# Latent attention: the maxima of a pair of heads taken ahead of the sums of the pair before

## The chip, the cores and the metric
The kernel runs on one core of a Trainium2 chip. The metric is the time of one execution on the device in microseconds (us), the median of a few runs.

## What is computed
The reference is a trunk of four residual layers over 256 tokens of width 1024 in float32: RMSNorm, a token mixer, RMSNorm, a SwiGLU channel mixer with 2816 hidden columns. The mixers are stick-breaking attention (layers 0 and 3), multi-head latent attention (layer 1) and sliding-window attention (layer 2). The change touches layer 1 alone:

```
def block(args):                      # 16 heads, CHUNK = 64
    logits = (einsum('bqhd,bshd->bhqs', qn, k_nope) + einsum('bqhr,bsr->bhqs', qr, k_rope)) * scale
    logits = where(key_chunk[None, :] <= q_chunk[:, None], logits, NEG_INF)
    p = softmax(logits, axis=-1)
    return einsum('bhqs,bshd->bqhd', p, v)
```

and the result of the heads goes through the output projection `w_o` and is added to x.

## The kernel before
All products of weights are made on TensorE in three passes: a weight unit w (128 x 2048 float32, 1 MB) is taken apart into a high part `w_hi` (ScalarE, L458) and a low part `w_lo = raw - w_hi` (VectorE, L783). There are 183 such units besides the first three, streamed through three slots. SyncE loads unit u into slot u mod 3 once VectorE has taken the low part of unit u-3; TensorE waits for `lo_done`. In the code both engines call this step `split(u)`. Units b to b+7 of layer 1 (b is its first unit) are projections down and up, units b+8 to b+11 its output projection.

The engines run programs written out by hand, one queue for each engine in program order, tied by semaphores. In layer 1 the 16 heads go as 8 pairs, p = 0 to 7. For a pair there are these steps:

- TensorE `logits(p)`: mask, early queries (128 keys) and late queries (256 keys) of both heads into one of two double banks. It waits for `exps(p-2)`, which empties that double bank.
- VectorE `maxima(p)`: two reductions from the banks (L984, L985) and the scaled negative (L987).
- ScalarE `exps(p)`: four exponentials into `scratch` (L599). They wait for `maxima(p)`.
- VectorE `sums(p)`: two reductions over `scratch` (L994, L996) and the reciprocal (L998). They wait for `exps(p)`.
- GpSimd `mla_products`: four scalings of the exponentials in place (L387). They wait for the reciprocal.
- TensorE `transposes(p)`: three for each of two heads (L1500) into the one double bank 3. They wait for the copy of the pair before, the first three for two of the four products, the second three for all four.
- ScalarE `copy_pt(p)`: the transposed weights to SBUF (L607).
- TensorE `values(p)` (L1515): waits for the copy and for the low part of the output of pair p-2.
- ScalarE `out_hi(p)` (L612), VectorE `lo(p)` (L857): high and low part of the pair's output, in `o_split`.

TensorE's round is `transposes(p)`, `logits(p+3)`, `values(p-1)`; in round 0 `queries(7)` (24 tile products ending a projection) stands in between, in rounds 5 and 6 four tiles of the output projection follow, and in round 7 two. Below, "the projection's start" is the first tile of the output projection, behind `values(4)`. VectorE's `queries(7)` (L959) moves the last two heads' queries out of the bank. Before the rounds come `exps(0)` to `exps(2)`, `maxima(0)`, `maxima(1)`, `sums(0)`, `sums(1)`.

The first loop below is ScalarE's round, the second VectorE's:

```
                for p in range(PAIRS_OF_HEADS):
                    copy_pt(p)
                    if p >= 1:
                        out_hi(p - 1)
                    exps(p + 3)
...
                    sums(p + 2)
                    maxima(p + 3)
                    if p >= 1:
                        lo(p - 1)
                    if p in (2, PAIRS_OF_HEADS - 3):
                        split(b + 9 if p == 2 else b + 10)
```

The order of the instructions on each engine is this text; no planner moves anything.

Of the kernel before, what the change touches and what calls it, by code (L numbers as in the profile page):

```python
# [38 lines left out]
PAIRS_OF_HEADS = HEADS // 2  # L39
# [65 lines left out]
def trunk(nc, w, x_in, consts, gains, bv, rel_rows, rel_scratch, out):  # L105
    ctx = ExitStack()
    with ctx:
# [76 lines left out]
        def mla_scores(p):  # L184

            return two_banks[2 - p % 2][:, :].rearrange("p (a s) -> p a s", a=2)

        def mla_weights(p):
            return scratch[:, 768 * (p % 4):768 * (p % 4) + 768].rearrange("p (a s) -> p a s", a=2)

        def mla_turned(p):
            return turned[:, p % 2, :].rearrange("p (a s) -> p a s", a=2)

        def mla_out(p):
            return bank[(p + 1) % 2]
# [247 lines left out]
        def _(act):  # L443
# [7 lines left out]
            def split(u):  # L451

                if u >= UNITS:
                    return
                slot = u % RAW_SLOTS
                act.wait_ge(raw_loaded[slot], 16 * (u // RAW_SLOTS))
                act.wait_ge(unit_used, u - SPLIT_SLOTS + 1)
                act.activation(w_hi[slot][:, :], raw[slot][:, :], ACT.Copy).then_inc(hi_done, 1)  # L458
# [13 lines left out]
            def first_guess(s, count, first, last):  # L472

                act.wait_ge(s.ms, count)
                t = step(act.activation(guess[:, first:last], ms[:, first:last], ACT.Ln))
                act.wait_ge(act_step, t)
                act.activation(guess[:, first:last], guess[:, first:last], ACT.Exp, scale=-0.5).then_inc(s.guess, 1)
# [72 lines left out]
            def latent_attention(i):  # L550
                m, b, n, c = mixer[i], MIXER_BASE[i], 2 * i, latent

                def latent_hi(k):
                    act.wait_ge(c.c_new, k // 2 + 1)
                    act.activation(lat_hi[:, k, :], lat[:, k, :], ACT.Identity,
                                   scale=vec[:, G_CQ + k:G_CQ + k + 1]).then_inc(c.hi, 1)

                split(b + 3)
                first_guess(norm, n + 1, 0, SEQ + TOKEN_SUMS[n])
                for k in (0, 1, 3):  # L560
                    latent_hi(k)
                split(b + 4)
                first_guess(c, 1, SEQ, 514)
                for k in (4, 5):
                    latent_hi(k)

                act.wait_ge(m.krope_sum, 1)
                act.activation(k_all[HD:P, 0, :], bank[0][HD:P, 0:SEQ], ACT.Copy).then_inc(m.krope_new, 1)
                act.wait_ge(m.krope_new, 1)
                act.dma_start(k_all[HD:P, 1:HEADS, :],  # L570
                              k_all[HD:P, 0:1, :].to_broadcast([HD, HEADS - 1, SEQ])).then_inc(m.kfill, 16)
                split(b + 5)

                def value_part(t, half):

                    if t and half:
                        act.wait_ge(unit_used, b + 5)
                    else:
                        act.wait_ge(m.v_part, 2 * t + half + 1)
                    act.activation(v_all[:, t, 512 * half:512 * half + 512], bank[MLA_V_BANKS[2 * t + half]][:, :],  # L580
                                   ACT.Identity, scale=rstd_c[:, 512 + t:513 + t]).then_inc(m.v_new, 1)

                act.wait_ge(c.rstd, 1)
                value_part(0, 0)
                first_guess(c, 2, 0, SEQ)
                value_part(0, 1)
                split(b + 6)
                value_part(1, 0)
                value_part(1, 1)
                split(b + 7)  # L590

                def exps(p):
                    if p >= PAIRS_OF_HEADS:
                        return
                    pr, s, lg = mla_weights(p), small[:, p % 4, :], mla_scores(p)
                    act.wait_ge(m.max_new, 3 * p + 3)
                    for late, keys in enumerate((slice(0, P), slice(P, 384))):
                        for a in range(2):
                            act.activation(pr[:, a, keys], lg[:, a, keys], ACT.Exp,  # L599
                                           bias=s[:, 4 + 2 * late + a:5 + 2 * late + a],  # L600
                                           scale=MLA_SCALE).then_inc(m.exp_new, 1)

                def copy_pt(p):
                    act.wait_ge(m.pt, p + 1)
                    if p >= 2:
                        act.wait_ge(m.av, p - 1)
                    act.activation(mla_turned(p), two_banks[3][:, :].rearrange("p (a s) -> p a s", a=2)[:, :, 0:384],  # L607
                                   ACT.Copy).then_inc(m.pt_new, 1)

                def out_hi(p):  # L610
                    act.wait_ge(m.av, p + 1)
                    act.activation(o_hi[:, p, :], mla_out(p)[:, 0:SEQ], ACT.Copy).then_inc(m.o_hi, 1)  # L612

                split(b + 8)
                exps(0)
                exps(1)
                split(b + 9)
                exps(2)
                for p in range(PAIRS_OF_HEADS):
                    copy_pt(p)  # L620
                    if p >= 1:
                        out_hi(p - 1)
                    exps(p + 3)
                    if p == PAIRS_OF_HEADS - 3:
                        split(b + 10)
                out_hi(KT - 1)
                out_projection(i)
# [133 lines left out]
            for i in range(DEPTH):  # L761
                (stick_breaking, latent_attention, window_attention)[i % 3](i)
                swiglu(i)
# [4 lines left out]
        def _(dve):  # L768
# [8 lines left out]
            def split(u):  # L777

                if u >= UNITS:
                    return  # L780
                slot = u % RAW_SLOTS
                dve.wait_ge(hi_done, u + 1)
                dve.tensor_tensor(w_lo[slot][:, :], raw[slot][:, :], w_hi[slot][:, :].bitcast(FP32),  # L783
                                  ALU.subtract).then_inc(lo_done, 1)
# [127 lines left out]
            def latent_attention(i):  # L912
                m, b, n, c = mixer[i], MIXER_BASE[i], 2 * i, latent
# [63 lines left out]
                def maxima(p):  # L977
                    if p >= PAIRS_OF_HEADS:
                        return
                    s, lg = small[:, p % 4, :], mla_scores(p)  # L980
                    dve.wait_ge(m.logits, p + 1)
                    if p >= 4:
                        dve.wait_ge(m.p_new, 4 * (p - 3))
                    dve.tensor_reduce(s[:, 0:2], lg[:, :, 0:P], AX_X, ALU.max).then_inc(m.max_new, 1)  # L984
                    dve.tensor_reduce(s[:, 2:4], lg[:, :, P:384], AX_X, ALU.max).then_inc(m.max_new, 1)  # L985
                    dve.wait_ge(m.max_new, 3 * p + 2)
                    dve.tensor_scalar(s[:, 4:8], s[:, 0:4], -MLA_SCALE, None, ALU.mult).then_inc(m.max_new, 1)  # L987

                def sums(p):
                    if p >= PAIRS_OF_HEADS:  # L990
                        return
                    s, pr = small[:, p % 4, :], mla_weights(p)
                    dve.wait_ge(m.exp_new, 4 * p + 2)
                    dve.tensor_reduce(s[:, 8:10], pr[:, :, 0:P], AX_X, ALU.add).then_inc(m.sum_new, 1)  # L994
                    dve.wait_ge(m.exp_new, 4 * p + 4)
                    dve.tensor_reduce(s[:, 10:12], pr[:, :, P:384], AX_X, ALU.add).then_inc(m.sum_new, 1)  # L996
                    dve.wait_ge(m.sum_new, 2 * p + 2)
                    dve.reciprocal(s[:, 12:16], s[:, 8:12]).then_inc(m.inv_new, 1)  # L998

                def lo(p):  # L1000
                    dve.wait_ge(m.o_hi, p + 1)
                    out_lo(m, o_lo[:, p, :], mla_out(p)[:, 0:SEQ], o_hi[:, p, :])
# [7 lines left out]
                queries(5)  # L1010
                queries(6)
                sums(1)
                maxima(2)
                split(b + 8)
                for p in range(PAIRS_OF_HEADS):
                    if p == 1:
                        queries(7)
                    sums(p + 2)
                    maxima(p + 3)
                    if p >= 1:  # L1020
                        lo(p - 1)
                    if p in (2, PAIRS_OF_HEADS - 3):
                        split(b + 9 if p == 2 else b + 10)
                lo(KT - 1)
                out_projection(i)

# [810 lines left out]
```

## Time and profile before

| | |
|---|---|
| median of 3 runs | 1195.81 us (1195.05 to 1196.33) |
| the profiled execution: own time | 1196.22 us |
| its span, first to last instruction | 1194.2 us |
| TensorE busy | 98% of the span |
| VectorE, ScalarE, GpSimd busy | 68%, 53%, 24% |
| mean granted clock of TensorE | 0.996 |

The span is the part of the execution that the trace shows; the profiled execution's own time is about 2 us more. Times in the rows below count from the start of the span. A matmul's end is modelled, so the starts are the safer numbers. A row of the timeline may merge several equal instructions (xN), and then its length is that of the whole group.

### The profile page before, as it was taken

Reading aid. Unit: us, or ns where it says so; the run is one execution under the profiler, and the core shown is the slowest. Engines: PE = TensorE matmul, PEld = TensorE weight load, DVE = VectorE, ACT = ScalarE, POOL = GpSimd, SP = SyncE. Lnnn points to the kernel's source line nnn. Section 1 sums busy time; section 2 is a strip of 40 time slices with the busy share of each in tenths; the row PEclk is TensorE's granted clock in tenths of the full one; section 3 lists DMA queues with packets and bytes.
Section 4 is the critical chain, followed back from the end, with each engine's and each line's share of the span. In section 5 each row is a group of like instructions: output and inputs, shape, how many; then the busy total and the mean of one; then the engine's idle time right before and its main releaser. Section 6 shows DMA issues by size and latency. Waiting matters only on the chain.

```text
span 1194.2 us, 18227 instructions
## 1 busy us (share of the span) xinstructions
PE 1168.3 (98%) x7410; PEld 1040.5 (87%) x7410; DVE 810.5 (68%) x857; ACT 628.3 (53%) x763; POOL 286.5 (24%) x290
## 2 busy tenths in 40 slices
PE   8999999999999999999999999999999999999996
PEld 6988888888998888888899888888889888888885
DVE  7686767775588667776556577766556867777653
ACT  5675565554354555554436545555346755555531
POOL 5000542211123343221101153221110005422221
PEclk9999999999999999999999999999999999999999
DMA  9733545555552345555543245555545324455541
GB/s 314 217 121 106 176 177 180 180 206 194 186 174 89 114 160 212 180 182 206 194 156 107 82 170 212 183 201 201 187 160 193 106 106 177 177 193 187 196 165 35
DMA packets 30828, 201.84 MB, mean 169 GB/s; under 512 B 3504, under 2 KB 4592, under 8 KB 7328
## 3 DMA queue, kind: packets, MB, share of 16 engines
q1 hardware_dynamic: 28800, 197.41, 46.9%
q0 software_dynamic: 352, 1.31, 0.9%
q10 hardware_dynamic: 1600, 2.02, 0.7%
q8 instruction: 58, 0.95, 0.3%
q14 instruction: 18, 0.15, 0.0%
HBM read 197.91 MB, written 1.84 MB: 167 GB/s over the span
## 4 chain that ended last, share of the span: by engine, by line
PE 89%; DVE 8%; ACT 2%; DMA 0%; issue 0%; DVEq 0%; ACTq 0%
PE banks L1209 39%; PE banks L1213 21%; PE banks L1203 6%; PE banks L1205 6%; PE banks L1204 6%; PE banks L1197 4%; DVE w_lo L783 3%; DVE x_split L798 2%; PE banks L1338 1%; PE banks L1280 1%; PE banks L1352 1%; PE banks L1582 1%; DVE w_lo L792 1%; PE banks L1610 0%; ACT w_hi L458 0%; PE banks L1340 0%
## 5 line engine op out<-in xcount | busy, mean ns | idle before, releaser
L783 DVE TENSOR_TENSOR w_lo<-raw,w_hi 128x2048 fp32r<-128x2048 f32 x183 | 450.4, 2461 | 214.0 <-ACT w_hi L458 213.9
L458 ACT ACTIVATE w_hi<-raw 128x2048 fp32r<-128x2048 f32 x183 | 349.3, 1909 | 97.0 <-PE banks L1213 47.2
L1209 PE MATMUL banks<-x_split,w_hi 128*128 128x512 f32 x1408 | 339.1, 392 | 5.5 <-DVE x_split L798 5.4
L1209 PEld LDWEIGHTS banks<-x_split,w_hi 128*128 128x128 f32 x1408 | 258.6, 188 | 58.7 <-DVE x_split L798 8.9
L1213 PEld LDWEIGHTS banks<-x_split,w_lo 128*128 128x128 f32 x1408 | 181.8, 192 | 6.9
L1213 PE MATMUL banks<-x_split,w_lo 128*128 128x256 f32 x1408 | 184.0, 284 | 0.0
L1209 PE MATMUL banks<-hid_split,w_hi 128*128 128x512 f32 x704 | 173.2, 392 | 0.0
L1209 PEld LDWEIGHTS banks<-hid_split,w_hi 128*128 128x128 f32 x704 | 127.4, 188 | 23.3
L1203 PE MATMUL banks<-x_split,w_hi 128*128 128x256 f32 x384 | 110.3, 287 | 0.0
L1204 PE MATMUL banks<-x_split,w_hi 128*128 128x256 f32 x384 | 108.6, 283 | 0.0
L1205 PE MATMUL banks<-x_split,w_lo 128*128 128x256 f32 x384 | 108.6, 283 | 0.0
L353 POOL TENSOR_TENSOR scratch<-scratch,rstd 128x512 f32<-128x512 f32 x44 | 57.4, 1305 | 205.8 <-ACT scratch L712 205.8
L356 POOL TENSOR_TENSOR scratch<-scratch 128x512 f32<-128x512 f32 x44 | 71.8, 1631 | 140.2 <-DVE scratch L1122 139.9
L1213 PEld LDWEIGHTS banks<-hid_split,w_lo 128*128 128x128 f32 x704 | 94.0, 191 | 5.8
L338 POOL TENSOR_TENSOR sq<-x 128x256 f32<-128x256 f32 x62 | 57.5, 927 | 163.0 <-DVE x_split L798 127.6
L1213 PE MATMUL banks<-hid_split,w_lo 128*128 128x256 f32 x704 | 95.6, 282 | 0.0
L1203 PE MATMUL banks<-o_split,w_hi 128*128 128x256 f32 x320 | 92.6, 289 | 0.4
L1205 PE MATMUL banks<-o_split,w_lo 128*128 128x256 f32 x320 | 90.5, 283 | 0.0
L1204 PE MATMUL banks<-o_split,w_hi 128*128 128x256 f32 x320 | 90.5, 283 | 0.0
L470 ACT ACTIVATE x_split<-x,vec 128x256 fp32r<-128x256 f32 x64 | 30.7, 503 | 108.9 <-DVE x L1154 81.7
L700 ACT ACTIVATE scratch<-banks 128x512 f32<-128x512 f32 x44 | 26.2, 596 | 115.5 <-PE banks L1213 115.5
L1203 PEld LDWEIGHTS banks<-x_split,w_hi 128*128 128x128 f32 x384 | 73.5, 191 | 2.8 <-issue 2.4
(174 smaller groups left out, 1476.9 us busy)
## 6 DMA issues: line engine op xcount, KB each, us to landing
raw<-w SPq DMA_DIRECT2D x183, 1024.0 KB, 4.9
raw<-w SPq DMA_DIRECT2D x8, 256.0 KB, 6.3
x<-x_in SPq DMA_DIRECT2D x2, 512.0 KB, 5.5
raw<-w SPq DMA_DIRECT2D x2, 512.0 KB, 8.4
out<-x SPq DMA_DIRECT2D x4, 256.0 KB, 2.9
k_all<-k_all ACTq DMA_DIRECT2D x1, 960.0 KB, 10.5
rel_scratch<-rel_lut POOLq DMA_DIRECT2D x1, 768.0 KB, 10.6
rel_bias<-rel_scratch POOLq DMA_DIRECT2D x2, 256.0 KB, 8.5
```

Of the source, the lines that this page charges most:

```text
L338: step(pool.tensor_tensor(dst[:, :], x[:, k, :], x[:, k, :], ALU.mult))
L353: pool.tensor_tensor(gate, gate, both(rstd[:, 0:SEQ]), ALU.mult).then_inc(f.scaled, 1)
L356: pool.tensor_tensor(value, gate, value, ALU.mult).then_inc(f.hid, 1)
L458: act.activation(w_hi[slot][:, :], raw[slot][:, :], ACT.Copy).then_inc(hi_done, 1)
L470: act.activation(x_hi[:, k, :], x[:, k, :], ACT.Identity, scale=gain(n, k)).then_inc(norm.hi, 1)
L783: dve.tensor_tensor(w_lo[slot][:, :], raw[slot][:, :], w_hi[slot][:, :].bitcast(FP32), ALU.subtract).then_inc(lo_done, 1)
L1197: ins = pe.matmul(dst, a, v, start=first and n == 0, stop=last and n == 2, skip_group_check=True)
L1203: pe.matmul(dst, wh, xh, start=first, stop=False, skip_group_check=True)
L1204: pe.matmul(dst, wh, xl, start=False, stop=False, skip_group_check=True)
L1205: return pe.matmul(dst, wl, xh, start=False, stop=last, skip_group_check=True)
L1209: return pe.matmul(pair(b), wt[0], xs, start=first, stop=False, skip_group_check=True)
L1213: return pe.matmul(pair(b)[:, 1, :], wt[1], xs[:, 0, :], start=False, stop=last, skip_group_check=True)
```

## The change
On VectorE each round takes `maxima(p+3)` ahead of `sums(p+2)` instead of behind it, and the round p = -1 takes `maxima(2)` alone. `queries(7)` goes from the start of round 1 to the end of round 0. The low part of unit b+8 goes from ahead of the rounds to the end of round 1, that of b+9 from the end of round 2 to the end of round 3; that of b+10 stays at the end of round 5. On ScalarE `exps(p+3)` goes ahead of `out_hi(p-1)`. No instruction is added or removed, and TensorE's, GpSimd's and SyncE's programs are the same.

```diff
@@ -618,9 +618,9 @@
                 exps(2)
                 for p in range(PAIRS_OF_HEADS):
                     copy_pt(p)
+                    exps(p + 3)
                     if p >= 1:
                         out_hi(p - 1)
-                    exps(p + 3)
                     if p == PAIRS_OF_HEADS - 3:
                         split(b + 10)
                 out_hi(KT - 1)
@@ -1010,17 +1010,16 @@
                 queries(5)
                 queries(6)
                 sums(1)
-                maxima(2)
-                split(b + 8)
-                for p in range(PAIRS_OF_HEADS):
-                    if p == 1:
+                for p in range(-1, PAIRS_OF_HEADS):
+                    maxima(p + 3)
+                    if p >= 0:
+                        sums(p + 2)
+                    if p == 0:
                         queries(7)
-                    sums(p + 2)
-                    maxima(p + 3)
                     if p >= 1:
                         lo(p - 1)
-                    if p in (2, PAIRS_OF_HEADS - 3):
-                        split(b + 9 if p == 2 else b + 10)
+                    if p in (1, 3, PAIRS_OF_HEADS - 3):
+                        split({1: b + 8, 3: b + 9}.get(p, b + 10))
                 lo(KT - 1)
                 out_projection(i)
```

## Rows read from the trace of the kernel before

**Rows 1.** The page, parts 1 and 4: TensorE busy; the chain by engine.
```profile
PE 1168.3 (98%) x7410; PEld 1040.5 (87%) x7410; DVE 810.5 (68%) x857; ACT 628.3 (53%) x763; POOL 286.5 (24%) x290
...
PE 89%; DVE 8%; ACT 2%; DMA 0%; issue 0%; DVEq 0%; ACTq 0%
```

**Rows 2.** Busy time by windows, from pair 1's transposes to the output projection.
```profile
core 0: us, PE busy (x) PEld busy (x) DVE busy (x) ACT busy (x) POOL busy (x), PEclk, DMA share, GB/s
373.88:391.97 18.09, 14.62 (x121) 10.64 (x119) 15.70 (x35) 9.41 (x25) 7.83 (x20) 1.00 0.34 117
```

**Rows 3.** Timeline of TensorE: start us, us, instruction, [idle before, releaser].
```profile
371.30 0.60 PE L1488 MATMUL banks<-k_all,q_all 128*128 128x256 f32 x2
...
373.88 0.81 PE L1500 MATMUL banks<-table,scratch 128*128 128x128 f32 x6
...
376.22 0.87 PE L1515 MATMUL banks<-turned,v_all 128*64 128x256 f32 x8
...
377.76 0.87 PE L1500 MATMUL banks<-table,scratch 128*128 128x128 f32 x6 [0.67 <-ACT turned L607]
...
381.37 0.87 PE L1500 MATMUL banks<-table,scratch 128*128 128x128 f32 x6 [0.34 <-ACT turned L607]
...
385.43 0.87 PE L1500 MATMUL banks<-table,scratch 128*128 128x128 f32 x6 [0.79 <-ACT turned L607]
...
390.36 0.87 PE L1500 MATMUL banks<-table,scratch 128*128 128x128 f32 x6 [1.67 <-ACT turned L607]
...
391.97 0.39 PE L1203 MATMUL banks<-o_split,w_hi 128*128 128x256 f32 x1
```

**Rows 4.** Timeline of VectorE in the same stretch.
```profile
371.10 2.28 DVE L783 TENSOR_TENSOR w_lo<-raw,w_hi 128x2048 fp32r<-128x2048 f32 x1
...
373.30 0.41 DVE L994 TENSOR_REDUCE small<-scratch 128x2 f32<-128x256 f32 x1
...
374.43 0.39 DVE L984 TENSOR_REDUCE small<-banks 128x2 f32<-128x256 f32 x1
...
375.53 0.68 DVE L959 TENSOR_TENSOR q_all<-banks,rope_q 128x512 f32<-128x512 f32 x1
...
383.19 0.41 DVE L857 TENSOR_TENSOR o_split<-banks,o_split 128x256 fp32r<-128x256 f32 x1
...
383.52 2.28 DVE L783 TENSOR_TENSOR w_lo<-raw,w_hi 128x2048 fp32r<-128x2048 f32 x1
```

**Rows 5.** Timeline of ScalarE in the same stretch.
```profile
372.45 0.83 ACT L607 ACTIVATE turned<-banks 128x768 f32<-128x768 f32 x1
...
375.66 1.35 ACT L599 ACTIVATE scratch<-banks,small 128x128 f32<-128x128 f32 x4 [2.37 <-DVE small L987]
...
376.88 0.83 ACT L607 ACTIVATE turned<-banks 128x768 f32<-128x768 f32 x1
...
377.57 0.41 ACT L612 ACTIVATE o_split<-banks 128x256 fp32r<-128x256 f32 x1
```

**Rows 6.** Timeline of GpSimd: the four products of pairs 1 and 2.
```profile
370.00 3.72 POOL L387 TENSOR_SCALAR scratch<-scratch,small 128x128 f32<-128x128 f32 x4 [1.87 <-DVE small L998]
374.61 1.62 POOL L387 TENSOR_SCALAR scratch<-scratch,small 128x128 f32<-128x128 f32 x4 [0.89 <-DVE small L998]
```

**Rows 7.** Timeline in the channel mixer of layer 1: VectorE and GpSimd.
```profile
449.25 2.28 DVE L783 TENSOR_TENSOR w_lo<-raw,w_hi 128x2048 fp32r<-128x2048 f32 x1
...
449.48 3.21 POOL L356 TENSOR_TENSOR scratch<-scratch 128x512 f32<-128x512 f32 x1 [3.51 <-DVE scratch L1122]
```

**Rows 8.** Windows (columns as Rows 2) at the entries of two channel mixers.
```profile
132.00:136.00 4.00, 2.62 (x11) 1.52 (x9) 2.85 (x6) 1.60 (x3) 3.61 (x6) 1.00 0.77 262
...
136.00:138.00 2.00, 1.85 (x9) 1.77 (x10) 0.85 (x2) 1.22 (x1) 1.84 (x3) 0.73 0.00 0
...
138.00:140.00 2.00, 2.00 (x12) 2.00 (x11) 1.54 (x1) 0.00 (x0) 2.00 (x1) 0.50 0.00 0
...
420.00:424.00 4.00, 3.30 (x14) 2.17 (x12) 3.07 (x6) 0.83 (x2) 3.61 (x6) 1.00 0.65 219
```

## The prediction

> **What bounds the kernel now.** I read the page first. TensorE is busy 98% of the span and is 89% of the chain that ended last; loads have no share in it [rows 1]. A reordering in layer 1 can therefore only win what TensorE waits there. The windows give it: from the transposes of pair 1 (373.88) to the projection's start (391.97) TensorE is busy 14.62 of 18.09 us at the full clock, and VectorE 15.70 [rows 2]. The timeline shows where. Each of the transposes of pairs 2 to 5 has idle time ahead of it, released by ScalarE's copy [rows 3]. A round without a wait is as long as transposes, logits and values: 376.22 - 373.88 = 2.34 for the first two and 0.80 for the values, 3.14 us. The last stretch, from 390.36 to 391.97, is 1.61. So 18.09 - 4 x 3.14 - 1.61 = 3.9 us are waits, and that is the most that can be won. Behind 391.97 TensorE has projection tiles between its steps for pairs, and I count nothing there.
>
> Why is the copy late? ScalarE has `exps(p+2)` ahead of `copy_pt(p)`: the copy of pair 1 starts at 376.88, behind the exponentials of 375.66, though its transposes began at 373.88 [rows 3, 5]. Those exponentials waited for maxima that stood behind sums on VectorE: 374.43 behind 373.30, and these behind a low part of 2.2 us at 371.10 [rows 4]. The change cuts this tie. I see it as real: sums of a pair need its exponentials, and the next pair's maxima don't.
>
> **Durations.** Start to next start: sums 1.13 (373.30 to 374.43), maxima 1.10 (374.43 to 375.53), a low part of weights 2.20 (371.10 to 373.30), `lo` 0.33 (383.19 to 383.52) [rows 4]. From the start of maxima to the exponentials 1.25 (374.43 to 375.66, rounded up), exponentials 1.22 (375.66 to 376.88), `out_hi` 0.41 long and its `lo` 0.44 behind its start; a copy 0.70 to the next and 0.88 to the transposes (376.88 to 377.76) [rows 3 to 5]. From sums to the products on GpSimd 1.31 (373.30 to 374.61), and the products 1.62 [rows 4, 6]. Logits: transposes 0.66, then 1.68 to the values, and 1.79 from their start to the maxima, an estimate from 371.30 + 0.60.
>
> **The term that speaks against the change.** The four products of pair 1 took 3.72 us and not 1.62; VectorE's low part of b+8 lay over them, 371.10 to 373.38 [rows 4, 6]. In the channel mixer a GpSimd product started 0.23 behind such a low part and ended 1.29 behind its end (449.48 + 3.21 against 449.25 + 2.28) [rows 7]. So the low part of a unit and a GpSimd instruction exclude one another; what GpSimd has left when it starts comes 2.2 us later. The Trainium skill, "SBUF — State Buffer", section "Who interferes with whom", states this as a rule: one pair of ports is an exclusive lock between GpSimd and a VectorE instruction with two SBUF inputs, held for the whole instruction. The low part reads `raw` and `w_hi`, so by that rule it contends; the trace agrees, with the 3.72 us.
>
> In the kernel before, maxima stand between the sums and the low part of b+9, so its products (of pair 4) are through before 383.52, and the collision of b+8 at 371.10 lies under TensorE's `queries(7)`, which ends only at 373.88. After the change the low parts of b+8 and b+9 stand directly behind sums and `lo`, and the products just released are half done.
>
> **Round by round, after the change.** Logits of pair 3 end at 371.90, so `maxima(3)` starts 371.93 and `exps(3)` 373.18 (375.66 before). `sums(2)` 373.03, products of pair 2 374.34 to 375.96, `queries(7)` 374.16 to 374.85. This last is moved at no cost: VectorE then idles for the logits of pair 4, which start 0.66 behind TensorE's 373.88.
> Round 1: `copy_pt(1)` waits for its transposes, 374.73; values(0) 376.22; transposes(2) 377.02 (377.76 before, gain 0.74). `maxima(4)` 376.33, `exps(4)` 377.59, `sums(3)` 377.47, products(3) from 378.78. `out_hi(0)` stands behind the exponentials, 378.82, so `lo(0)` 379.26, and the low part of b+8 comes at 379.59, where two of four products are through. They end at about 382.7, behind 381.8 to 382.2 when the low part ends. That is the first collision.
> Round 2: TensorE could start transposes(3) at 380.17 and has the first three; the second three wait until 382.8. Logits(6) 383.2, values(2) 384.9. VectorE has `maxima(5)` only at 381.85 and `exps(5)` is at 383.08, `sums(4)` 382.95, products(4) 384.26 to 385.88. `copy_pt(3)` comes behind `out_hi(1)` at 384.58.
> Round 3: transposes(4) 385.69 (385.43 before), the second three at 386.0; logits(7) 386.4, values(3) 388.1. `maxima(6)` 385.08, `exps(6)` 386.33, `sums(5)` 386.20, products(5) from 387.51; `out_hi(2)` 387.56, `lo(2)` 388.00, low part of b+9 388.33 to 390.6 or, behind a third product, 390.95. Second collision: the products end at 391.4.
> Round 5: transposes(5) may start at 388.9, but the second three wait for the last product, 391.5. Values(4) 391.9, the projection's start 392.7. Before it was 391.97 [rows 3]: **0.7 us later.**
>
> Behind that everything TensorE asks for is ready: `maxima(7)` 390.6 and `exps(7)` 391.85, products(6) to 394.6 for transposes asked for at 395.7, products(7) hit by the low part of b+10 (396.25) until 399.1, against 400.2. The first tiles of the projection want `o_lo` of pair 3 at 394.9 and have it at 393.9. So its rhythm, and all behind it, moves as one.
>
> **Moved edits that cost nothing.** The low part of b+8 ends 8.5 us later and that of b+9 about 5 later, and SyncE's loads of b+11 and of the next mixer's first unit with them. TensorE needs b+8 at the projection's start and b+9 some 4.5 us on; b+11 follows behind all of both, far over 10 us later. With the late ends of 382 and 391 there are 10 and 6 us to spare; without that cover each us of lateness would be one of the end. GpSimd has no DMA in layer 1, so its queue carries only products. `out_hi` behind the exponentials delays `lo(p-1)` by 1.2 us, and values of pair p+1 wait for it; in round 2 they start at 384.9 with `lo(0)` done at 379.6. The queue behind the waiting `lo` is the low part, 0.66 us in round 1 and 0.67 in round 3; only by that do two products get through first.
>
> **The unknown prices.** How the lock goes at a tie: the third product first or the low part first. It moves the end of the low part by 0.4 and the products' end hardly, so +0.4 to +1.3 for the forecast with my rounding of each step. Whether the second product pair is held: if all four got through, round 5's wait would be gone; if none did, transposes(5) start late as a whole, 0.3 more.
>
> **Rivals.**
> No collision that binds (18%): GpSimd's products slip through before the low part, as in the kernel before at 383.52, because `lo` waits longer than I have it. It decides if the low part of b+9 starts 0.8 us later than 388.33. Transposes(3) would be whole at 380.2, transposes(4) at 385.46 (VectorE's 2.2 us at b+8 still delay `exps(5)`), transposes(5) 388.8 with all products at 389.13, the projection at 390.35: -1.6 us, 1194.2.
> Full pipelining (4%): maxima stay so far ahead that all waits go, -3.9 us, 1191.9. VectorE speaks against it, 15.70 of 18.09 us busy, with both low parts still in the stretch [rows 2].
> A fall of TensorE's clock (16%): the clock granted was 0.73 and 0.50 in 136 to 138 and 138 to 140 us, behind a stretch in which TensorE was busy 2.62 of 4 us; a like entry at 420 to 424 with 3.30 of 4 kept 1.00 [rows 8]. The fall took (1 - 0.73) x 2 + (1 - 0.50) x 2 = 1.5 us of matmul time at least. The change makes two waits of 2.3 us where the longest was 1.67 [rows 3]; if one of them brings the half clock to the projection, that is 0.7 + 1.5 = +2.2, 1198.0, and two falls, or one whole with the late tie, +2.6 to +3.8. It decides if the granted clock is under 1 between 383 and 397. Against it: at 388.7 the wait of 1.67 did nothing.
> The change does nothing (10%): both orders meet the same last wait, within 0.3 of before. Near the forecast in time, and not to be told from it but by the trace.
>
> **How the numbers follow.** The forecast, two collisions and +0.4 to +1.3, has 52%. Profiled execution: 1196.22 with a span of 1194.2, so 1196.9 and 1194.9 after. The median before was 0.4 lower than the profiled one; I put 0.7 on the median: 1195.81 + 0.7 = 1196.5. The range takes in the no-collision case below with the runs' own spread of 0.6, and one clock fall above with the same: 1193.7 to 1198.8. A measurement tells about 0.2%, 2.4 us, from no change. Faster by that needs over 60% of all waits gone: full pipelining and a small part of the no-collision case, 5%. Slower by that: the worse part of the clock case, 10%. The same 85%.
>
> **What the profile after would show.** Products of pairs 3 and 5 at 3.6 to 3.9 us and that of pair 4 at 1.62: the collisions. `exps(3)` 2.5 us earlier: the cut tie. TensorE's longest idle inside the transposes of pairs 3 and 5, its releaser no longer ScalarE's copy but GpSimd's product; the projection's start near 392.7. I am wrong if that start is before 391.5 (the products weren't held or not waited for), or if it is after 394 (a wait that I don't see), or if the clock falls there.

## The result and the profile after

Measured together, 20 runs of each: the kernel before 1195.12 us in the median (1194.43 to 1196.75), the changed kernel 1196.94 us (1195.71 to 1199.30). The ratio is 1.0014, with a 95% interval of 1.0008 to 1.0020: 1.7 us slower, inside what the prediction called the same, and inside its range. The profiled execution took 1198.20 us, its span 1196.3 us.

The page after has GpSimd on the chain that ended last, with 1%, where it had no share [rows 1]:

```profile
PE 1171.4 (98%) x7410; PEld 1042.7 (87%) x7410; DVE 809.8 (68%) x857; ACT 628.7 (53%) x763; POOL 291.9 (24%) x290
...
PE 90%; DVE 7%; ACT 2%; POOL 1%; DMA 0%; issue 0%; DVEq 0%; ACTq 0%
```

The stretch from the transposes of pair 1 to the projection's start, by windows (columns as in [rows 2]). It was 18.09 us and is 20.11, and VectorE's work in it is nearly the same, 15.61 us against 15.70 [rows 2]. TensorE is busy 16.70 us for the work that took 14.62, at a mean clock of 0.90:

```profile
373.07:393.18 20.11, 16.70 (x120) 11.69 (x118) 15.61 (x32) 9.55 (x25) 10.71 (x16) 0.90 0.20 64
```

The same stretch on TensorE's timeline answers to [rows 3]:

```profile
373.07 0.82 PE L1499 MATMUL banks<-table,scratch 128*128 128x128 f32 x6
...
376.21 0.87 PE L1499 MATMUL banks<-table,scratch 128*128 128x128 f32 x6
...
379.41 0.55 PE L1499 MATMUL banks<-table,scratch 128*128 128x128 f32 x3
381.75 0.55 PE L1499 MATMUL banks<-table,scratch 128*128 128x128 f32 x3 [1.79 <-POOL scratch L387]
...
386.23 0.87 PE L1499 MATMUL banks<-table,scratch 128*128 128x128 f32 x6
...
389.43 0.55 PE L1499 MATMUL banks<-table,scratch 128*128 128x128 f32 x3
391.59 0.55 PE L1499 MATMUL banks<-table,scratch 128*128 128x128 f32 x3 [1.61 <-POOL scratch L387]
...
393.18 0.58 PE L1202 MATMUL banks<-o_split,w_hi 128*128 128x256 f32 x1
```

The reader is to see two things. Transposes of pair 2 follow at once, without the 0.67 of before. And those of pairs 3 and 5 are cut in two halves of three, with a wait in between that a GpSimd product ends. The copy from ScalarE ends no wait any more. VectorE's, ScalarE's and GpSimd's timelines of the changed kernel show why:

```profile
378.78 2.30 DVE L783 TENSOR_TENSOR w_lo<-raw,w_hi 128x2048 fp32r<-128x2048 f32 x1
381.01 0.41 DVE L984 TENSOR_REDUCE small<-banks 128x2 f32<-128x256 f32 x1
...
388.62 2.30 DVE L783 TENSOR_TENSOR w_lo<-raw,w_hi 128x2048 fp32r<-128x2048 f32 x1
```

```profile
372.39 1.35 ACT L599 ACTIVATE scratch<-banks,small 128x128 f32<-128x128 f32 x4
373.93 0.81 ACT L607 ACTIVATE turned<-banks 128x768 f32<-128x768 f32 x1 [0.19 <-PE banks L1499]
```

```profile
377.96 3.73 POOL L387 TENSOR_SCALAR scratch<-scratch,small 128x128 f32<-128x128 f32 x4 [2.77 <-DVE small L998]
383.44 1.62 POOL L387 TENSOR_SCALAR scratch<-scratch,small 128x128 f32<-128x128 f32 x4 [1.74 <-DVE small L998]
387.81 3.73 POOL L387 TENSOR_SCALAR scratch<-scratch,small 128x128 f32<-128x128 f32 x4 [2.74 <-DVE small L998]
...
395.41 3.76 POOL L387 TENSOR_SCALAR scratch<-scratch,small 128x128 f32<-128x128 f32 x4 [0.50 <-DVE small L998]
```

`exps(3)` comes 0.68 us ahead of the start of transposes(1) where it came 1.78 behind it [rows 3, 5]: 2.5 us sooner. The low parts of 378.78 and 388.62 lie over the products of pairs 3 and 5, which take 3.73 us; those of pair 4 take 1.62. The last line is pair 7's products, held by the low part of b+10 as the prediction had it; TensorE asks for them only at 401.87 and doesn't wait. The granted clock (columns as in [rows 2]) is what the single timelines don't say:

```profile
376.00:380.00 4.00, 3.96 (x35) 2.74 (x31) 3.36 (x7) 2.33 (x6) 2.04 (x3) 1.00 0.03 6
380.00:384.00 4.00, 2.25 (x12) 1.88 (x13) 3.37 (x8) 1.75 (x6) 2.26 (x4) 0.78 0.42 123
384.00:388.00 4.00, 4.00 (x28) 2.79 (x28) 2.62 (x7) 1.96 (x6) 1.26 (x4) 0.79 0.33 139
388.00:392.00 4.00, 2.38 (x18) 1.40 (x17) 3.68 (x6) 0.96 (x2) 3.54 (x4) 1.00 0.00 0
392.00:396.00 4.00, 4.00 (x23) 3.40 (x22) 2.98 (x9) 3.90 (x8) 2.22 (x6) 0.57 0.76 266
```

This trace had no fall of the clock at the entry of layer 0's channel mixer, where that of before had one [rows 8], but one of 10 to 14 us from the span's start, and its layer 1 starts 0.8 us sooner. Below I therefore count from the start of transposes(1), which the change doesn't move (it stands 4.39 us behind that of transposes(0) in both traces), to the projection's start and to the end of the span. "Falls" are stretches of lower clock behind transposes(1), the last 12 us of the span left aside; in windows of 2 us the granted clock goes down to 0.50 to 0.56 in each of them, the lower of its two levels (1.2 and 2.4 GHz). The kernels of the table are explained in the next section.

| kernel | to the projection | to the end | falls | ratio to before, 95% |
|---|---|---|---|---|
| before | 18.09 | 820.3 | 0 | |
| changed | 20.11 | 823.2 | 2 | 1.0014 (1.0008 to 1.0020) |
| changed, again | 20.87 | 823.5 | 2 | |
| old places | 18.02 | 820.1 | 1 | 0.9993 (0.9985 to 1.0002) |
| one input | 18.05 | 820.1 | 1 | 0.9999 (0.9990 to 1.0008) |
| ScalarE as before | 18.22 | 820.3 | 0 | 1.0008 (1.0000 to 1.0017) |
| filler 16 | 21.49 | 823.5 | 0 | 1.0029 (1.0019 to 1.0039) |
| filler 8 | 18.68 | 822.4 | 1 | 1.0014 (1.0005 to 1.0023) |
| filler 8, again | 18.68 | 820.7 | 0 | |
| b+9 away | 16.58 | 819.1 | 0 | 0.9995 (0.9986 to 1.0004) |
| before, colliding | 19.50 | 821.5 | 1 | 1.0008 (0.9999 to 1.0017) |
| before, 0.7 us more | 18.98 | 821.1 | 0 | 1.0009 (1.0000 to 1.0018) |
| clear | 14.41 | 816.9 | 0 | 0.9975 (0.9966 to 0.9984) |
| clear, b+9 early | 14.41 | 818.8 | 1 | 0.9973 (0.9962 to 0.9984) |

Each count stands for one profiled execution; the ratios stand for 7 to 20 timed runs of the kernel, and 0.0010 of them is 1.2 us.

### The profile page after: what moved, and what is told of

Read it like the earlier page. It is cut to its first block, busy times and chain, and to the rows that moved or that the text cites. A ratio compares the mean times of both kernels' runs of the same rounds, so it can differ in the third digit from the quotient of the medians.

```text
span 1196.3 us, 18227 instructions
## 1 busy us (share of the span) xinstructions
PE 1171.4 (98%) x7410; PEld 1042.7 (87%) x7410; DVE 809.8 (68%) x857; ACT 628.7 (53%) x763; POOL 291.9 (24%) x290
## 4 chain that ended last, share of the span: by engine, by line
PE 90%; DVE 7%; ACT 2%; POOL 1%; DMA 0%; issue 0%; DVEq 0%; ACTq 0%
PE banks L1208 39%; PE banks L1212 21%; PE banks L1202 6%; PE banks L1204 6%; PE banks L1203 6%; PE banks L1196 4%; DVE w_lo L783 2%; DVE x_split L798 2%; PE banks L1337 1%; PE banks L1279 1%; PE banks L1351 1%; PE banks L1581 1%; POOL scratch L387 1%; DVE w_lo L792 1%; PE banks L1487 1%; PE banks L1609 0%
## 5 line engine op out<-in xcount | busy, mean ns | idle before, releaser
L338 POOL TENSOR_TENSOR sq<-x 128x256 f32<-128x256 f32 x62 | 61.7, 996 | 163.0 <-DVE x_split L798 127.6
```

Source lines behind the costliest of these rows:

```text
L338: step(pool.tensor_tensor(dst[:, :], x[:, k, :], x[:, k, :], ALU.mult))
```

## The experiments

All of them change layer 1 alone.

**Old places.** The changed order, with the low parts of b+8 and b+9 where they were.

```diff
                 for p in range(-1, PAIRS_OF_HEADS):
                     maxima(p + 3)
+                    if p == -1:
+                        split(b + 8)
...
-                    if p in (1, 3, PAIRS_OF_HEADS - 3):
-                        split({1: b + 8, 3: b + 9}.get(p, b + 10))
+                    if p in (2, PAIRS_OF_HEADS - 3):
+                        split(b + 9 if p == 2 else b + 10)
```

> The changed order of maxima and sums, with the low parts of b+8 and b+9 where they were (ahead of round 0, and at the end of round 2). Lock theory (a low part and GpSimd's products exclude one another, and TensorE waits for the held products): the products of pair 4 take 3.7 us, those of pairs 3 and 5 1.6 us; one wait of TensorE on a product instead of two; the projection's start 1.6 us earlier than before, so -1.6 us against before, or about 0 if the clock falls behind that one wait. Theory that the order of maxima and sums itself costs: slower than before by 1 to 2 us, as the changed kernel is. Theory that ScalarE's order costs: the same, 1 to 2 us slower.

GpSimd's and TensorE's timelines of this kernel:

```profile
377.54 1.63 POOL L387 TENSOR_SCALAR scratch<-scratch,small 128x128 f32<-128x128 f32 x4 [1.48 <-DVE small L998]
380.79 3.74 POOL L387 TENSOR_SCALAR scratch<-scratch,small 128x128 f32<-128x128 f32 x4 [1.62 <-DVE small L998]
```

```profile
384.59 0.55 PE L1501 MATMUL banks<-table,scratch 128*128 128x128 f32 x3 [1.85 <-POOL scratch L387]
```

One collision that TensorE waits for, with pair 4, and one wait; transposes(5) follow at 389.07. With one fall of the clock behind the wait, the projection starts 18.02 us behind transposes(1), and not 16.5. The order of maxima and sums itself costs nothing: the ratio is 0.9993 (0.9985 to 1.0002). Its lowest three runs, 1192.93 to 1193.19, are 1.2 us under the lowest of before (1194.10), which is about what a run without that fall would give.

**One input.** The low parts of b+8 and b+9 are not computed; a reduction over `raw` of the same length stands in their place.

```diff
+                def one_input(u):
+                    slot = u % RAW_SLOTS
+                    dve.wait_ge(hi_done, u + 1)
+                    dve.tensor_reduce(w_lo[slot][:, 0:1], raw[slot][:, :], AX_X, ALU.max).then_inc(lo_done, 1)
...
-                    if p in (1, 3, PAIRS_OF_HEADS - 3):
-                        split({1: b + 8, 3: b + 9}.get(p, b + 10))
+                    if p in (1, 3):
+                        one_input(b + 8 if p == 1 else b + 9)
+                    if p == PAIRS_OF_HEADS - 3:
+                        split(b + 10)
```

> The changed kernel, but the low parts of b+8 and b+9 are not computed: a reduction over raw of the same 2048 columns stands in their place, with one SBUF input instead of two and the same waits and signals. Lock theory: all products take 1.6 us, TensorE no longer waits for a product, the clock stays at 1.00, and the kernel is 1.6 us faster than before (3.4 us faster than the changed one). Theory that only VectorE's queue counts (2.2 us ahead of maxima 5 and 7 whatever the instruction is): no change against the changed kernel, +1.8 us against before.

VectorE's, GpSimd's and TensorE's timelines and one window:

```profile
379.74 2.27 DVE L1003 TENSOR_REDUCE w_lo<-raw 128x1 fp32r<-128x2048 f32 x1
```

```profile
378.92 1.63 POOL L387 TENSOR_SCALAR scratch<-scratch,small 128x128 f32<-128x128 f32 x4 [2.76 <-DVE small L998]
384.37 1.63 POOL L387 TENSOR_SCALAR scratch<-scratch,small 128x128 f32<-128x128 f32 x4 [3.81 <-DVE small L998]
387.62 1.63 POOL L387 TENSOR_SCALAR scratch<-scratch,small 128x128 f32<-128x128 f32 x4 [1.62 <-DVE small L998]
```

```profile
385.57 1.39 PE L1506 MATMUL banks<-table,scratch 128*128 128x128 f32 x6 [1.93 <-POOL scratch L387]
```

```profile
384.00:388.00 4.00, 2.43 (x12) 2.10 (x13) 2.85 (x9) 3.08 (x10) 2.01 (x6) 0.74 0.53 221
```

The instruction in the low part's place begins as far behind the sums and is as long (2.27 us), yet products(3) and (5) take 1.63 us. So it is not VectorE being busy that shuts GpSimd out. The reduction is also another operation and writes one column where the low part writes 2048; that neither of these makes the difference is seen in the kernel before, where `queries(7)` (375.53 to 376.21), a TENSOR_TENSOR with one input from the bank `banks` and one from SBUF that writes 512 columns, lay over the products of pair 2, and they took 1.62 us [rows 4, 6]. What is left is the second input from SBUF. That much of the expectation held. The gain of 1.6 us did not come: the ratio is 0.9999. The 2.2 us ahead of `maxima(5)` and `sums(4)` are still there, products(4) start only at 384.37, and TensorE waits 1.93 us for them; behind that wait the clock fell in this trace, and the stretch is 18.05 us, 1.6 longer than the 16.5 of the prediction's no-collision case. That case had the wait too (transposes(4) at 385.46, which is 11.58 us behind transposes(1); here 11.54), but gave the fall no place in it.

**ScalarE as before.** The changed kernel with `out_hi(p-1)` ahead of `exps(p+3)`.

```diff
                     copy_pt(p)
-                    exps(p + 3)
                     if p >= 1:
                         out_hi(p - 1)
+                    exps(p + 3)
```

> The changed kernel with ScalarE's order as before (out_hi ahead of the exponentials). Lock theory: lo comes up to 0.8 us earlier and the low parts with it, so that they hold three products or four instead of two; the waits on products stay, two of 1.5 to 2.3 us; 0 to -0.7 us against the changed kernel, +1 to +2 against before. Theory that ScalarE's order costs: the loss against before goes, +0.3 or less.

```profile
377.04 3.66 POOL L387 TENSOR_SCALAR scratch<-scratch,small 128x128 f32<-128x128 f32 x4 [2.76 <-DVE small L998]
...
385.38 3.66 POOL L387 TENSOR_SCALAR scratch<-scratch,small 128x128 f32<-128x128 f32 x4 [1.81 <-DVE small L998]
```

```profile
380.04 0.52 PE L1499 MATMUL banks<-table,scratch 128*128 128x128 f32 x3 [1.49 <-POOL scratch L387]
```

(GpSimd's and TensorE's timelines.) The low part starts at 377.17, 0.13 us behind the products, and they are held almost whole, but it is over sooner too, and at each of the two pairs TensorE waits some 1.5 us ahead of the first three transposes and 0.2 ahead of the second, where it waited 1.79 and 1.61. From transposes(1) to the projection 18.22 us, no fall in this trace. In the runs it is 0.7 us better than the changed kernel, with overlapping intervals. The interval, 1.0000 to 1.0017, holds both what the lock theory expected against before (+1 to +2 us) and what the theory on ScalarE's order did (+0.3 or less), so the runs don't decide. In the traces the order is worth 0.5 us against filler 8 below, which has the same two collisions and no fall in layer 1 either (18.22 against 18.68); the rest of the 1.9 us to the changed kernel's 20.11 comes with the falls.

**Filler 16 and filler 8.** More matmuls in both waits, so that TensorE is not idle there.

```diff
                     for a in range(2):
+                        if a == 1 and p in (3, 5):
+                            for _ in range(FILL):
+                                pe.matmul(bank[6][:, 384:512], ident, x[:, 0, 0:P], start=True, stop=True)
                         pe.wait_ge(m.p_new, 4 * p + 2 * a + 2)
```

> The changed kernel with 16 more matmuls of 128 columns (about 1.8 us, into columns that nobody reads) ahead of the second three transposes of pairs 3 and 5, that is inside TensorE's two waits on products. Clock theory (half of the loss is not the waits but the half clock behind them): the clock stays at 1.00 in this stretch, the waits on the product shrink to some 0.3 us, and the kernel is 1 to 1.5 us faster than the changed one, +0.3 to +0.9 against before, with a smaller spread of its runs. Theory that the waits alone cost: no change or up to 0.3 us slower than the changed kernel.

```profile
380.52 3.74 PE L1500 MATMUL banks<-x,table 128*128 128x128 f32 x32
```

(TensorE's timeline.) I had sized them by the transposes, six in 0.66 us. They take twice that, 3.74 us for 16, longer than the waits. So the kernel is slower than the changed one, 1.0029, and not the 1 to 1.5 us faster that were expected. The trace says one thing: with TensorE busy the clock stayed at 1.00 through layer 1. With 8 of them the size is right:

> As the filler kernel, with 8 matmuls instead of 16: they took 3.74 us for 16, so 1.9 us for 8, which lies inside the waits of 2.1 to 2.3 us. Clock theory: granted clock 1.00 in layer 1, the projection's start 0.7 to 0.9 us later than before counted from the transposes of pair 1, and so +0.7 to +0.9 against before, 0.9 to 1.1 us faster than the changed kernel. Theory that the waits alone cost: as the changed kernel, +1.8.

> The kernel with 8 filler matmuls in each wait once more. Clock theory: granted clock 1.00 from 376 to 400 us again, and the loss that is left over 0.7 us stands at an entry of a channel mixer.

The windows of the second profile of filler 8 in layer 1, then the one of its first profile, in layer 3, where the clock fell:

```profile
380.00:384.00 4.00, 4.00 (x35) 3.63 (x34) 3.90 (x7) 1.13 (x4) 2.31 (x2) 1.00 0.25 57
384.00:388.00 4.00, 4.00 (x31) 2.68 (x31) 2.82 (x8) 3.08 (x9) 2.31 (x6) 1.00 0.49 207
...
392.00:396.00 4.00, 4.00 (x38) 3.70 (x32) 2.49 (x7) 4.00 (x7) 2.71 (x7) 1.00 0.59 242
```

```profile
1002.00:1008.00 6.00, 5.53 (x25) 5.07 (x26) 3.40 (x3) 3.27 (x3) 4.84 (x5) 0.72 0.19 37
```

Both traces have 18.68 us to the projection, 0.6 more than before, and no fall in layer 1. One has none later either and ends 0.4 us over before (820.7 against 820.3); the other has one at layer 3's channel mixer and ends 1.7 us later. So in the traces the rest of the changed kernel's loss, 2.5 and 2.8 us (823.2 and 823.5 against the 820.7 of the filler without any fall), comes with its two falls. The timed runs don't follow: I had expected filler 8 to be 0.9 to 1.1 us faster than the changed kernel, and its ratio is the same 1.0014. Its mean clock over 11 runs is 0.9957, that of before 0.9956 and that of the changed kernel 0.9947.

**The changed kernel again**, for the place of its falls.

> The changed kernel once more, for where its clock falls. Clock theory: granted clock under 1 once or twice between 382 and 396 us, as in its first profile. If these falls are chance, none here.

```profile
380.00:384.00 4.00, 2.87 (x13) 2.44 (x14) 3.09 (x8) 2.34 (x6) 2.25 (x6) 0.64 0.57 186
384.00:388.00 4.00, 4.00 (x30) 2.81 (x28) 2.41 (x7) 1.80 (x6) 1.07 (x3) 0.93 0.18 76
388.00:392.00 4.00, 2.21 (x17) 1.30 (x18) 3.97 (x7) 0.86 (x3) 3.11 (x3) 0.92 0.14 23
392.00:396.00 4.00, 4.00 (x25) 3.29 (x26) 2.56 (x7) 4.00 (x8) 2.63 (x7) 0.65 0.63 244
```

Again two falls, in nearly the same two stretches. I don't take their places for chance. But not every run can have had both as they are here. In all 14 traces transposes(1) start at 372.1 us or later, so a run with both falls would have a span of at least some 372.1 + 823.2 = 1195.3 us (an estimate); 11 of the 20 timed runs of the changed kernel have a shorter one, 1193.6 to 1195.0. Both profiled executions, 1196.3 and 1196.0, are from its slower half.

**Before, 0.7 us more.** The kernel before with three more matmuls ahead of the projection.

```diff
                         pe.wait_ge(m.exp_new, 4 * 7)
+                        for _ in range(3):
+                            pe.matmul(bank[4][:, 0:P], ident, x[:, 0, 0:P], start=True, stop=True)
                         out_part(i, 0, range(0, 4))
```

> The kernel before with three more matmuls of 128 columns (0.7 us, result not read) ahead of the output projection's first tile in layer 1: the same lateness at the projection's start as the changed kernel's own, with none of its waits. Theory that the loss is the lateness and the clock falls in layer 1: +0.7 us in the median against before, mean clock as before. Theory that any such shift moves the later entries of the channel mixers to where the clock falls more often: +1.5 to +2.2 us in the median, though TensorE's added work is 0.7 us; the lowest run at +0.7.

```profile
390.71 0.94 PE L1538 MATMUL banks<-x,table 128*128 128x128 f32 x6
391.40 0.36 PE L1203 MATMUL banks<-o_split,w_hi 128*128 128x256 f32 x1
```

(TensorE's timeline.) They take 0.69 us; the other 0.2 of the stretch's 0.89 came ahead of them, at transposes(2), where TensorE waited 0.86 instead of 0.67. The trace ends 0.8 us later, with no fall; the lowest run is 1195.06 against 1194.10, and the ratio 1.0009 with 1.0000 to 1.0018. That spans both expectations, 0.7 us and 1.5 or more. Inconclusive on whether a shift of this size brings more falls at later entries.

**b+9 away.** The changed kernel with the low part of b+9 at the end of round 5 and that of b+10 at the end of round 6.

```diff
-                    if p in (1, 3, PAIRS_OF_HEADS - 3):
-                        split({1: b + 8, 3: b + 9}.get(p, b + 10))
+                    if p in (1, 5, 6):
+                        split({1: b + 8, 5: b + 9}.get(p, b + 10))
```

> The changed kernel with only the low part of b+9 moved away, to the end of round 5 (b+10 to the end of round 6). Lock theory: the products of pair 5 take 1.6 us, those of pair 3 stay at 3.7; one wait on a product instead of two; the projection's start 1.6 us earlier than before, with one fall of the clock behind the first wait 0 against before, without it -1.6. Theory that the first collision (b+8) makes the loss: as the changed kernel, +1 to +2.

```profile
382.38 0.55 PE L1499 MATMUL banks<-table,scratch 128*128 128x128 f32 x3 [1.79 <-POOL scratch L387]
```

(TensorE's timeline.) One wait is left, at transposes(3), and the stretch is 16.58 us, 1.5 shorter than before, where 1.6 were expected without a fall. The ratio, 0.9995 (0.9986 to 1.0004), is between the two numbers, 0 and -1.6 us. Against the changed kernel's 1.0014 the second collision carries the loss: what the first one costs is less than what the new order gains by pair 5.

**Before, colliding.** The kernel before, with the low part of b+9 between the sums of pair 4 and the maxima of pair 5.

```diff
                     sums(p + 2)
+                    if p == 2:
+                        split(b + 9)
                     maxima(p + 3)
                     if p >= 1:
                         lo(p - 1)
-                    if p in (2, PAIRS_OF_HEADS - 3):
-                        split(b + 9 if p == 2 else b + 10)
+                    if p == PAIRS_OF_HEADS - 3:
+                        split(b + 10)
```

> The kernel before, with the low part of b+9 directly behind the sums of pair 4 instead of behind maxima(5) and lo(1). Lock theory: the products of pair 4 take 3.8 us or start 2.2 us late, but maxima(5) is late by the same 2.2 us and decides; transposes of pair 4 start 1.6 us later, those of pair 5 some 0.6 us later: +0.6 against before, and up to +2.1 if the clock falls behind the wait of 2.4 us. Theory that only the wait on ScalarE's copy counts and the place of a low part doesn't: within 0.3 us of before.

```profile
379.91 3.58 POOL L387 TENSOR_SCALAR scratch<-scratch,small 128x128 f32<-128x128 f32 x4 [1.98 <-DVE small L998]
```

```profile
385.27 1.54 PE L1502 MATMUL banks<-table,scratch 128*128 128x128 f32 x6 [2.37 <-ACT turned L607]
```

(GpSimd's and TensorE's timelines.) The same exclusion in the old order: 3.58 us for pair 4's products. The wait that counts is the one on the copy, 2.37 us, with the clock at 0.65 from 384 to 388 behind it. 1.2 us more to the end and a ratio of 1.0008 (0.9999 to 1.0017): between its two numbers. The interval reaches down to what the other theory expected, within 0.3 us of before; against that theory stands the trace, with 19.50 us to the projection for 18.09.

**Clear, and clear with b+9 early.** The changed order with no low part where its held products are wanted soon: b+8 ahead of round 0 (as before), b+9 at the end of round 5, b+10 of round 6.

```diff
                 for p in range(-1, PAIRS_OF_HEADS):
                     maxima(p + 3)
+                    if p == -1:
+                        split(b + 8)
...
-                    if p in (1, 3, PAIRS_OF_HEADS - 3):
-                        split({1: b + 8, 3: b + 9}.get(p, b + 10))
+                    if p in (5, 6):
+                        split(b + 9 if p == 5 else b + 10)
```

> The changed order of maxima and sums; the low part of b+8 ahead of round 0, where queries(7) covers what it holds, that of b+9 at the end of round 5 and that of b+10 at the end of round 6, where the held products are wanted only 4 us later. Lock theory: no wait on a product ahead of the projection's start, transposes 3 to 5 follow one another at 3.2 us, 3.9 us gained there, some 0.2 lost where the projection's second unit waits for b+9: about -3.5 us against before, clock 1.00 in the stretch. Theory that the order of maxima and sums is worth nothing: -1 us or less.

A window of this kernel from transposes(1) to the projection, and its GpSimd timeline:

```profile
372.14:386.55 14.41, 14.41 (x121) 10.64 (x119) 12.24 (x33) 9.98 (x27) 6.50 (x16) 1.00 0.21 74
```

```profile
368.26 3.72 POOL L387 TENSOR_SCALAR scratch<-scratch,small 128x128 f32<-128x128 f32 x4 [1.87 <-DVE small L998]
...
377.03 1.62 POOL L387 TENSOR_SCALAR scratch<-scratch,small 128x128 f32<-128x128 f32 x4 [1.42 <-DVE small L998]
...
388.92 5.69 POOL L387 TENSOR_SCALAR scratch<-scratch,small 128x128 f32<-128x128 f32 x4 [0.49 <-DVE small L998]
```

TensorE is busy all of the 14.41 us at the full clock. The products of pair 1 are held for `queries(7)` to hide, those of pair 7 for 5.69 us by two low parts, under projection tiles. To the end it is 3.4 us less than before in the trace. The ratio is 0.9975 (0.9966 to 0.9984), or 3.0 us, with medians of 1192.37 against 1194.68; about 3.5 were expected. The slowest of its 11 runs, 1192.64, is under the fastest of before beside it, 1194.17, and under the fastest of the changed kernel's 20, 1195.71: a small gain, but clear of both kernels.

> The clear version with the low part of b+9 at the end of round 4 instead of 5. Lock theory: the products of pair 6 are held (3.7 us) and not those of pair 7 (5.7 us in the clear version), both under projection tiles; b+9 is ready 2.5 us sooner, and the 0.4 us go that TensorE waits for it ahead of the projection's second unit: 0.4 us faster than the clear version, unless the held products of pair 6 come up to 0.9 us late for their transposes.

Its edit against the clear version:

```diff
-                    if p in (5, 6):
-                        split(b + 9 if p == 5 else b + 10)
+                    if p in (4, 6):
+                        split(b + 9 if p == 4 else b + 10)
```

```profile
390.13 0.49 PE L1501 MATMUL banks<-table,scratch 128*128 128x128 f32 x3
391.20 0.55 PE L1501 MATMUL banks<-table,scratch 128*128 128x128 f32 x3 [0.59 <-POOL scratch L387]
```

(TensorE's timeline.) The held products are now those of pair 6 and TensorE waits for them: transposes(7) start 22.71 us behind transposes(1), in the clear version 22.33. The 0.4 us saved are paid back twice. So the version is not the 0.4 us faster that were expected, and its ratio, 0.9973, can't be told from the clear version's.

## Why the prediction was right, and where not

**The bound** held: at most 3.9 us were to be won between transposes(1) and the projection. The clear version won 18.09 - 14.41 = 3.7 there.

**The cut tie** held: `exps(3)` 2.5 us sooner, transposes(2) 0.7 sooner, no more waits on the copy.

**The collisions** held, by place and size: products(3) and (5) at 3.73 us (I said 3.6 to 3.9), those of pair 4 at 1.62. The experiment with one input shows the cause, and that of b+9 away shows that the second collision is the one that reaches the projection. The Trainium skill's "SBUF — State Buffer", section "Who interferes with whom", says that a VectorE instruction with two SBUF inputs contends with a GpSimd instruction that reads SBUF. The runs agree: two SBUF inputs 3.73 us, one input 1.63. That the hold lasts for the whole instruction stands in that section with VectorE's 2-port modes, not with two inputs; for the low part it is shown by the 3.73 us, 2.1 more than the 1.62 alone.

**The round-by-round sum** held where the clock did. The prediction had the projection 18.8 us behind transposes(1) (392.7 - 373.88); with the clock kept up by filler it is 18.68, twice, and to the end +0.4 against before, where the forecast had +0.4 to +1.3. For b+9 away the same arithmetic gives 16.5 and the trace 16.58. One small slip: by their own working the ends of the range come out as 1193.6 and 1198.6 and not 1193.7 and 1198.8, which changes nothing.

**The step that failed** is the weight of the clock rival. It gave a fall between 383 and 397 us 16% and let the likeliest case go without. Both profiles of the changed kernel have two falls, between 380 and 388 and between 388 and 396 us, each at one of the waits of 1.6 to 1.8 us that a product ends (the prediction's 2.3 is from the start of the first three transposes to the second three, 0.55 of which is work), and stand 2.5 and 2.8 us over the filler kernel's profile without a fall. By the sign that the prediction gave, a granted clock under 1 between 383 and 397 us, the trace is that of the rival and not of the forecast: +2.6 to +3.8 us for two falls, and the trace has 823.2 - 820.3 = +2.9. The argument against it, that the wait of 1.67 us before did nothing, was too weak: in the trace of the kernel with 0.7 us more the same wait, 1.67 us, again did nothing, but falls came at waits of 1.61, 1.78, 1.79 (twice), 1.85, 1.93 and 2.37 us, though not at that of 1.79 in b+9 away. What sets such waits apart no run shows. The median is only 0.4 us over the forecast, and that is in part luck: the medians lie 1.8 apart and not 0.7, while the median of before was 0.7 lower in 20 runs than in the three that the forecast started from.

**What stays open.** In the traces the two falls are the difference between +0.4 and +2.9. In the timed runs filler 8, whose mean clock is that of before, is as slow as the changed kernel. One part of the reason is seen in the spans: 11 of 20 runs of the changed kernel are too short for both falls, so its timed runs lose less than its traces. The other part isn't: without any fall outside the last microseconds filler 8 would have a span of some 372.1 + 820.7 = 1192.8 us (an estimate), and its shortest is 1193.3, the next 1194.3, while about half of the runs of before reach the 1192.4 that the same sum gives there. Falls elsewhere, as at layer 0's and layer 3's entries in its two traces, would fit, but no trace shows it of those runs. The mean clock can't tell: most runs of before have 0.996, in the faster and in the slower of their two groups. The run with 0.7 us more was to tell and its interval is too wide. So of the +1.7 us of the timed runs 0.4 to 0.6 are shown by the traces, as the net of the new order and its two collisions, and the clock's part is only argued. What the timed runs do show is the whole: the same order of maxima and sums is at 1.0014 with the low parts over products that TensorE waits for, and at 0.9975 with them away.

**The rivals.** No collision that binds: refuted by the 3.73 us; and the trace with one input shows that without the collision the gain of 1.6 can still be taken by the next wait and its fall. Full pipelining: not here, and VectorE speaks against it as the prediction said, with 15.61 us of work in the stretch. The clear version reaches it with the same instructions, but because neither the low part of b+8 (369.36) nor that of b+9 (389.05) lies between 372.14 and 386.55: VectorE has 12.24 of 14.41 us there. The change does nothing: refuted, by the trace's 20.11 for 18.09 and by the interval, 1.0008 to 1.0020.

## What to carry to other kernels

When VectorE's long two-input instructions are moved in a hand-written order, ask which GpSimd instruction has just been released: directly behind the sums that feed GpSimd is a bad place, behind work that GpSimd isn't waited for is the right one. Taking an operation ahead of its neighbour pays only if what stood between them isn't put on the path somewhere else: the same reordering gave a ratio of 1.0014 or of 0.9975, by the places of three low parts. And a wait of about 2 us on TensorE may cost more than itself, since the clock can fall behind it. Count from a mark that the change can't move, profile a kernel twice before a microsecond is explained, and ask whether the spans of the timed runs have room for what the profile shows.

## What the runs showed that I had not expected

- A float32 matmul of 128 columns in the filler takes 0.23 us (3.74 for 16, 0.69 for 3), a transpose of the same shape 0.11 (0.66 for six).
- Held products wait for more than one low part: 5.69 us instead of 1.62 with two in a row, 389.05 and 391.94, and `lo` in between.
- In the six traces with a fall of the clock at the entry of layer 0's channel mixer (136 to 142 us) transposes(1) start at 373.69 to 374.03 us, in the eight without it at 372.14 to 373.07. Six of those eight have a fall at 8 to 14 us instead; no trace has both. 32 runs of the kernel before lie in two groups, 1194.1 to 1194.6 and 1195.5 to 1196.6 us, the same 1.5 us apart, and its profiled execution, 1196.22 with that fall, is in the slower one. That the fall makes the groups is likely by this, but not shown.
